# Reordered norms and layer ends, token sums of squares, and zero matmuls in a two-layer f32 decoder trunk

## What is computed

```python
def rms_norm(x, g):
    y = x * lax.rsqrt(jnp.mean(x * x, axis=-1, keepdims=True) + NORM_EPS)
    return y * g
def modulate(x, g, shift, scale):
    return rms_norm(x, g) * (1 + scale[:, None, :]) + shift[:, None, :]
...
for i in range(2):
    sh1, sc1, g1, sh2, sc2, g2 = jnp.split(silu(c) @ ada_w[i] + ada_b[i], 6, axis=-1)
    h = modulate(x, tok_norm[i], sh1, sc1)
    y = short_conv_mixer(h, ...) if i == 0 else mla_mixer(h, ...)
    x = x + g1[:, None, :] * y
    h = modulate(x, ch_norm[i], sh2, sc2)
    x = x + g2[:, None, :] * peer_mixer(h, peer_q_w[i], peer_subkeys[i], peer_u[i], peer_v[i])
```

## Time and profile before

| what | value |
| --- | --- |
| median of 3 runs | 2018.03 us (2015.09 to 2019.81) |
| the profiled execution's own time | 2020.03 us |
| its span, first to last instruction | 2018.3 us |
| PE busy | 94% of the span |
| DVE, ACT, POOL busy | 81%, 50%, 14% |
| mean granted TensorE clock | 0.972 of full |
| DMA | 371.70 MB, mean 184 GB/s |

### The profile page before, as it was taken

One profiled execution on the slowest core, in us unless ns is written; L12 is line 12 of the kernel. 1 busy time (PEld: TensorE's weight loads), 2 busy tenths in 40 slices (PEclk: granted clock), 3 DMA queues, 4 the chain that ended last, 5 costly groups with the idle time before them and its releaser, 6 DMA issues.

```text
span 2018.3 us, 39416 instructions
## 1 busy us (share of the span) xinstructions
PE 1893.6 (94%) x12830; PEld 1650.6 (82%) x12830; DVE 1633.7 (81%) x3102; ACT 1008.4 (50%) x1620; POOL 292.5 (14%) x171
## 2 busy tenths in 40 slices
PE   2989899999999999999878889899999999999998
PEld 2988888888888888888766789898888888888876
DVE  6747999999999999987755469998888888888866
ACT  3334355555555555554433344445555555555543
POOL 2866500000000000000043167000000000000000
PEclk7999999999999999999878899999999999999999
DMA  7964544776777777777523045435555555555553
GB/s 284 336 230 139 171 147 144 221 223 225 219 227 225 223 220 228 221 219 235 169 65 98 35 154 158 141 119 181 183 178 178 179 178 182 179 177 179 183 180 132
DMA packets 102179, 371.70 MB, mean 184 GB/s; under 512 B 11344, under 2 KB 11728, under 8 KB 101584
## 3 DMA queue, kind: packets, MB, share of 16 engines
q1 hardware_dynamic: 94032, 341.26, 52.7%
q0 software_dynamic: 8064, 29.36, 5.0%
HBM read 369.53 MB, written 1.05 MB: 184 GB/s over the span
## 4 chain that ended last, share of the span: by engine, by line
PE 79%; DVE 13%; DVEq 3%; issue 1%; ACT 1%; DMA 1%; POOL 1%; SPq 0%; ACTq 0%; POOLq 0%
PE bank L506 35%; PE bank L492 17%; PE bank L494 9%; PE bank L422 4%; PE bank L423 4%; PE bank L424 4%; DVE w_lo L1030 2%; PE bank L518 2%; DVE hot_b L1265 1%; DVEq L1271 1%; PE bank L662 1%; DVE arena L1156 1%; DVE arena L1136 1%; POOL w_lo L986 1%; DVE arena L1123 1%
## 5 line engine op out<-in xcount | busy, mean ns | idle before, releaser
L727 ACT CAST w_hi<-raw 128x1024 fp32r<-128x1024 f32 (+1 forms) x603 | 630.8, 1046 | 311.7 <-PE bank L506 113.8
L1030 DVE TENSOR_TENSOR w_lo<-raw,w_hi 128x1024 fp32r<-128x1024 f32 x493 | 603.3, 1224 | 134.8 <-PE bank L494 59.7
L492 PE MATMUL bank<-act_two,w_hi 128*128 128x512 f32 x1536 | 548.1, 397 | 0.0
L494 PE MATMUL bank<-act_two,w_lo 128*128 128x256 f32 x1536 | 430.6, 280 | 0.0
L422 PE MATMUL bank<-act_two,w_hi 128*128 128x256 f32 x1092 | 321.0, 294 | 39.1 <-DVE w_lo L1030 17.1
L492 PEld LDWEIGHTS bank<-act_two,w_hi 128*128 128x128 f32 x1536 | 288.6, 188 | 69.0
L506 PE MATMUL bank<-w_hi,wt_hi 128*128 128x512 f32 x1024 | 328.2, 401 | 3.3 <-DVE wt_lo L1304 2.6
L506 PE MATMUL bank<-w_lo,wt_hi 128*128 128x512 f32 x1024 | 318.9, 393 | 0.0
L506 PE MATMUL bank<-w_hi,wt_lo 128*128 128x512 f32 x1024 | 316.1, 390 | 0.0
L423 PE MATMUL bank<-act_two,w_hi 128*128 128x256 f32 x1092 | 312.9, 287 | 0.0
L424 PE MATMUL bank<-act_two,w_lo 128*128 128x256 f32 x1092 | 312.5, 286 | 0.0
(11 more groups left out here) (212 smaller groups left out, 1915.0 us busy)
## 6 DMA issues: line engine op xcount, KB each, us to landing
raw<-in_u_panels SPq DMA_DIRECT2D x256, 512.0 KB, 3.6
raw<-in_v_panels SPq DMA_DIRECT2D x256, 512.0 KB, 3.6
raw<-in_panels SPq DMA_DIRECT2D x81, 512.0 KB, 4.1
ada<-in_ada_rows POOLq DMA_DIRECT2D x56, 512.0 KB, 4.7
arena<-in_ada_rows SPq DMA_DIRECT2D x40, 512.0 KB, 6.1
raw<-in_panels SPq DMA_DIRECT2D x6, 384.0 KB, 3.0
arena<-in_subkeys SPq DMA_DIRECT2D x2, 1024.0 KB, 5.6
xT<-in_xT SPq DMA_DIRECT2D x1, 1024.0 KB, 8.1
```

What stands on the lines that cost most here:

```text
L492: pe.matmul(bank[:, 0:2 * T], w_hi[:, slots[0], w], act_two[:, :, a], start=(k == 0), stop=False, skip_group_check=True)
L494: mm = pe.matmul(bank[:, 0:T], w_lo[:, slots[1], w], act_hi[:, a], start=False, stop=(k == KB - 1), skip_group_check=True)
L727: nc.scalar.copy(w_hi[:, slot, 0:width], raw[:, slot, 0:width]).then_inc(hi_done, 1)
L1030: dve.tensor_tensor(w_lo[:, lo_slot, 0:width], raw[:, slot, 0:width], w_hi[:, slot, 0:width].bitcast(F32), ALU.subtract).then_inc(lo_done, 1)
```

## The change

Seven edits in one:

- **Norm.** `square_sums` becomes `token_square_sums`: the squares are the stationary operand and one column of ones is streamed, so the sums stand with tokens on the partitions, one column for each tile of 128 tokens. Root and reciprocal then have 128x2 elements. `spread_rstd` brings the reciprocal back to all partitions with one matmul per tile (the reciprocal broadcast as stationary operand, the identity streamed) into STAT in PSUM, from where `scale_x` reads it. `block_square_sum` changes in the same way.
- **Opening.** Six slots for the rows instead of four; SP loads one row, then `xT`, constants and vectors, then the other rows; ACT writes silu straight to `silu_c`, and all rows read it there; POOL does its first `w_lo` after its multiplication by the reciprocal, which ACT copies from PSUM for it.
- **End of conv_in.** The last two rows, `modulation` and the release of `conv_out` change places: the gate of the last block and the release come first.
- **gains.** `gain` is computed in the stage before instead of at the start of `peer` and `attention`.
- **residual_panels.** The split of a panel goes ahead of the wait for the residual and its square.
- **Layer end.** A semaphore after tile 0's half of the last value panel; ACT copies tile 0 there and half of tile 1, DVE the other half. The output is stored in four parts as they are done.
- **busy.** Matmuls of 512 columns with a zero stationary and a zero streamed operand, into banks that nobody reads then: 38 in the opening; 4, 2 and 4 around the norm of each `peer`; 18 after each search; 2 ahead of each group of transposes in layer 0; 3, 2 and 4 around the norm of `attention`, 36 after its `first_pair`, 26 ahead of `q_b`.

```diff
-ADA = 4
+ADA = 6
...
-            for j in range(2):
-                load_ada(j, KB + j, j)
+            load_ada(0, KB, 0)
             sp.dma_start(xT[:], xT_in).then_inc(s_const, 16)
-            for j in range(2, ADA):
-                load_ada(j, KB + j, j)
             sp.dma_start(con[:, 0:C_MASK], con_in[:, 0:C_MASK]).then_inc(s_const, 16)
             sp.dma_start(vec[:], vec_in).then_inc(s_const, 16)
-            for j in range(ADA, KB):
+            for j in range(1, KB):
                 load_ada(j, KB + j, j % ADA)
...
-            sp.wait_ge(x_ready, 4)
-            sp.dma_start(out, xT[:]).then_inc(s_out, 16)
+            for t in range(TT):
+                for g in range(2):
+                    sp.wait_ge(yt_added, 4 + 2 * t + g + 1)
+                    part = lambda a: a.rearrange("p (k t) -> p k t", t=T)[:, 4 * g:4 * g + 4, t * P:(t + 1) * P]
+                    sp.dma_start(part(out), part(xT[:])).then_inc(s_out, 16)
...
-                        mm = pe.matmul(STAT[:, t * P:(t + 1) * P], ones, sq[:, t * D + k * P:t * D + (k + 1) * P],
+                        mm = pe.matmul(STAT[:, t:t + 1], sq[:, t * D + k * P:t * D + (k + 1) * P], ones[:, 0:1],
...
             def block_square_sum(n):
                 pe.wait_ge(sq_summed, n // 2)
-                pe.matmul(STAT[:, 0:T], ones, sq_sum, start=True, stop=False)
                 pe.wait_ge(sq_block, KB * n // 2)
-                pe.matmul(STAT[:, 0:T], ones, sq[:, (KB - 1) * T:KB * T], start=False, stop=True).then_inc(sum_ready, 1)
+                for t in range(TT):
+                    o = (KB - 1) * T + t * P
+                    pe.matmul(STAT[:, t:t + 1], sq_sum[:, t * P:(t + 1) * P], ones[:, 0:1], start=True, stop=False)
+                    mm = pe.matmul(STAT[:, t:t + 1], sq[:, o:o + P], ones[:, 0:1], start=False, stop=True)
+                mm.then_inc(sum_ready, 1)
+
+            def spread_rstd(n):
+                pe.wait_ge(rstd_ready, n)
+                for t in range(TT):
+                    mm = pe.matmul(STAT[:, T + t * P:T + (t + 1) * P], rstd[:, t:t + 1].broadcast_to([P, P]), ident,
+                                   start=True, stop=True)
+                mm.then_inc(rstd_spread, 1)
+
+            def busy(bank, count):
+                for _ in range(count):
+                    pe.matmul(bank[:], zero[:], zero[:].unsqueeze(1).broadcast_to([P, 4, P]), start=True, stop=True)
...
             def peer(l):
+                busy(SC[0], 4)
                 block_square_sum(2 * l + 2)
+                busy(SC[0], 2)
+                spread_rstd(2 * l + 2)
+                busy(SC[0], 4)
...
+                busy(STAT, 18)
...
             def attention():
-                square_sums(3)
+                busy(SC[0], 3)
+                token_square_sums(3)
+                busy(SC[0], 2)
+                spread_rstd(3)
+                busy(SC[0], 4)
                 for j in range(7):
                     if j == 0:
                         first_pair(norm_hi, norm_ready, 2 * KB, [wait_panel("mla_in", p) for p in range(2)])
+                        busy(SC[0], 36)
...
                 latent_sums(STAT, 2, QB, KVB)
+                busy(SC[0], 26)
                 pe.wait_ge(act_ready, 1)
...
-            square_sums(1)
+            token_square_sums(1)
+            spread_rstd(1)
+            busy(PAN[0], 38)
             first_pair(norm_hi, norm_ready, 0, [wait_panel("conv_in", p) for p in range(2)])
...
             def residual_panels(stage, after):
                 for i in range(KB):
+                    split_hi(*((stage, i + HI_LEAD) if i + HI_LEAD < KB else (after, i + HI_LEAD - KB)))
                     act.wait_ge(evac[stage], i + 3)
                     c = slice(i * T, (i + 1) * T)
                     nc.scalar.activation(sq[:, c], xT[:, c], ACT.Square).then_inc(sq_block, 1)
-                    split_hi(*((stage, i + HI_LEAD) if i + HI_LEAD < KB else (after, i + HI_LEAD - KB)))
...
-                act.wait_ge(pan_done, ring(f"last{l}", 31)[3] + HI)
+                act.wait_ge(y0_done, l + 1)
                 for n in range(2):
                     i = nc.scalar.mul(yrow[:, n * 512:(n + 1) * 512], YB[n][:], 1.0 / G_SCALE)
                 i.then_inc(y0_copied, 1)
+                act.wait_ge(pan_done, ring(f"last{l}", 31)[3] + HI)
+                nc.scalar.mul(yrow[:, 2 * 512:3 * 512], YB[2][:], 1.0 / G_SCALE).then_inc(y1_copied, 1)
...
-            split_lo("conv_in", 0)
             pool.wait_ge(s_const, 48)
-            pool.wait_ge(rstd0, 1)
+            pool.wait_ge(rstd0_copied, 1)
...
             def inverse_rms(n):
                 dve.wait_ge(rms_ready, n)
-                dve.reciprocal(rstd[:, 0:T], rms[:, 0:T])
+                dve.reciprocal(rstd[:, 0:TT], rms[:, 0:TT]).then_inc(rstd_ready, 1)
...
             def scale_x(n):
+                dve.wait_ge(rstd_spread, n)
                 for k in range(KB):
                     c = slice(k * T, (k + 1) * T)
+                    dve.scalar_tensor_tensor(out=act32[:, c], in0=xT[:, c], scalar=gain[:, k:k + 1], in1=STAT[:, T:2 * T],
+                                             op0=ALU.mult, op1=ALU.mult).then_inc(scaled, 1)
...
+                    if end:
+                        dve.sem_inc(evac["conv_out"], 2)
+                        for k in range(KB // 2, KB):
+                            conv_low(k)
+                        ada_row(17 + 3 * b, 12, it, 3 * b + 1)
+                        ada_row(15 + 12, 12, it, 11)
```

More of the change, by code:

```diff
@@ L507, in v_panel @@
                                                start=False, stop=False, skip_group_check=True)
+                    if t == 0 and tile0 is not None:
+                        mm.then_inc(tile0, 1)
                 mm.then_inc(pan_done, 1)
@@ L584, in peer @@
                         v_panel(f"last{l}", 2 * s + 1, 4, it, s, 1)
+                for s in range(2):
+                    pe.wait_ge(wt_ready, 64 * l + 48 + 14 + s + 1)
+                    v_panel(f"last{l}", 2 * s, 4, 7, s, 0)
+                    v_panel(f"last{l}", 2 * s + 1, 4, 7, s, 1, y0_done if s else None)
                 for t in range(TT):
-                    pe.wait_ge((y0_copied, y1_copied)[t], l + 1)
+                    if t == 0:
+                        pe.wait_ge(y0_copied, l + 1)
+                    else:
+                        pe.wait_ge(y1_copied, 2 * (l + 1))
                     for g in range(2):
+                        if l == 0:
+                            busy(YB[0], 2)
                         if 2 * t + g >= 2:
@@ L880, in _ @@
             act.wait_ge(s_c, 16)
+            nc.scalar.activation(silu_c, crow[:], ACT.Silu).then_inc(s_silu, 1)
             nc.scalar.activation(crow[:], crow[:], ACT.Silu).then_inc(s_silu, 1)
-            act.wait_ge(s_silu, 1)
-            nc.scalar.copy(silu_c, crow[:]).then_inc(s_silu, 1)
             act.wait_ge(s_const, 48)
@@ L1342, in experts @@
                     mix_body(q, 7, True)
+                if l == 0:
+                    gains(1, V_TOK + KB, 0)
                 def last_body(it, end):
@@ L1377, in peer @@
             def peer(l):
-                gains(l, V_CH + l * KB, 3)
                 inverse_rms(2 * l + 2)
-                scale_x()
+                scale_x(2 * l + 2)
                 normalised_lo(2 * l + 2, l, 3)
@@ L1417, in attention @@
             def attention():
-                gains(1, V_TOK + KB, 0)
                 dve.sem_inc(evac["mla_in"], 2)
                 inverse_rms(3)
-                scale_x()
+                scale_x(3)
                 normalised_lo(3, 1, 0)
@@ L1506, in attention @@
                 dve.sem_inc(qk_ready, 1)
+                dve.sem_inc(evac["mla_out"], 2)
+                gains(1, V_CH + KB, 3)
                 for i in range(HEADS + 3):
@@ L1585, in _ @@
                                                  op0=ALU.mult, op1=ALU.add)
-                    ada_row(17 + 3 * b, 12, it, 3 * b + 1)
-                    if b == 3:
-                        ada_row(15 + 12, 12, it, 11)
+                    end = b == 3 and it == 1
+                    if not end:
+                        ada_row(17 + 3 * b, 12, it, 3 * b + 1)
+                        if b == 3:
+                            ada_row(15 + 12, 12, it, 11)
                     dve.drain()
@@ L1598, in _ @@
                         conv_low(b)
-            for k in range(KB // 2, KB):
-                conv_low(k)
+            gains(0, V_CH, 3)
             add_to_x("conv_out", 0, 1)
```

50 lines of the change are left out of this document (24 added, 26 removed).

## The result

| | before | after |
| --- | --- | --- |
| median of 4 runs each, one chip | 2017.05 us (2015.09 to 2019.81) | 1991.74 us (1988.87 to 1995.65) |
| ratio | | 0.9875, 95% interval 0.9854 to 0.9896 |
| profiled execution, span | 2020.03, 2018.3 us | 1992.0, 1989.6 us |
| mean granted clock | 0.972 | 0.989 |

What follows compares the result with a forecast made beforehand. PE was taken as the bound, with some 1400 us of expert stages fixed and 640 us between where it waits or runs at half clock. Terms summed to 26.4 us: 2018.03 - 26.4 = 1991.6 us, range 1986 to 2003.

Steps and rivals of the forecast that it cites:

- Opening: Start to conv_in's panel 2: earlier constants, unblocked rows and full clock gain 10.5 us (8.5 to 11.5).
- End of conv_in: Earlier release leaves PE waiting 2.8 us for POOL's split; with half the half-clock window, gain 3.3 us (2 to 4.7).
- third rival: In conv_in, late loads take up to 5 us of the opening's gain: 1997 us, chance 5%.
- Starts of PEER: Both PEER stages: first product 1.0 us sooner and panel 0 ending 1.5 sooner; 3.0 us for both (1.2 to 4).
- Start of attention: Norm at the end of layer 0: shorter chain, scale_x 4.0 us sooner; 3.5 us arrive (1.5 to 4.2).
- at full clock only 16 records stand behind the last squares: Attention's norm: those records take 1.9 us, so the sums end at 1000.7 instead of 1003.50.
- Clock behind it: Behind attention's start and ahead of q_b, zeros avoid half-clock matmuls (2.5 and 1.7): 4.2 us (1 to 4.5).
- Small ones: Minor terms: mla_out released early 0.3, zeros behind the searches -0.2, the end of the run 1.8 us.
- The 18 zeros: Fillers behind each search, where PE waits for DVE's w_lo: nothing gained, -0.2 us (-2 to 0).
- End: End of the run: adds begin 1.1 us sooner and the last quarter's store saves 0.7; 1.8 us (1.0 to 2.7).
- second rival: Zeros do not count as activity, so PE drops to 0.50 inside the fillers: 2024 us, chance 4%.
- first rival: The clock falls all the same despite the zeros; only the chains count, 17.3 us: 2000.7 us, chance 13%.

Runs made afterwards that it cites:

- the wide norm: The changed kernel with the old 256-wide norms in front of both PEERs and attention, opening and zeros as in the change: 1998.06 us, ratio 0.9896.
- e4_gain_later: The changed kernel, but in the opening DVE computes the first gain after row 9 instead of before row 8: 1992.02 us, ratio 0.9862.
- e7_72: The changed kernel with 72 zero matmuls behind the first_pair of mla_in in place of 36: 1997.58 us, ratio 0.9888.
- e9_more_zeros: The changed kernel with zeros at four more places (conv_out's first_pair, attention's scores, its last value weights, mla_out): 1986.41 us, ratio 0.9841.
- e10_both: The changed kernel with sums streaming 128 columns, zeros at four more places, 46 opening zeros and 8 between first_pair's halves: 1984.54 us, ratio 0.9827.
- e12_all: The e10_both kernel with the first gain read from PSUM and 48 opening zeros: 1983.16 us, ratio 0.9821.

## Why the prediction was right

The time was right to 0.1 us, the gain to 1.1 (25.3 for 26.4), the terms less so. The profiles differ by 28.0 us, 2.7 more than the medians, so the measured terms add up to more than 26.4.

- **Opening**, 10.5: 10.4 measured. Order, loads and blocked gain came as worked out, and of the clock's share 0.6 (43.9 us without zeros) where 1.0 was forecast. The experiments add that the six slots are 2 us of it.
- **End of conv_in**, 3.3: 3.1, of which 0.6 lie in the loop. The third rival was there in small: the wait was 3.4 us, not 2.8, because of a load.
- **Starts of PEER**, 3.0: 1.9 each, 3.7. The chain from the last square to the first product went from 4.63 us to 3.64 in front of both, the 1.0 forecast, and at PEER 0 it did so without zeros too. The rest is first_pair at full clock, 8.23 us for 9.09: 0.9 each where I had 0.5. The zeros alone bring just that at PEER 0 (8.26).
- **Start of attention**, 3.5: 4.9 (1.0 of it ahead of the last transposes). The failed step is "at full clock only 16 records stand behind the last squares": the clock fell in the midst of the sums (981.61), they ended 2.9 us behind the last square instead of 2.0, and `scale_x` began 4.8 us behind it. Before it was 6.5, forecast was 3.3, and with 128 columns streamed, which held the clock, it is 3.4. So of 3.2 us this chain brought 1.7. That the term came in all the same was luck: the layer end brought what was missing. From the first transposes to the end of the last square pass 5.95 us for 8.24 (6.17 without zeros), and 1.0 lies ahead of them, where I had counted 0.75 for all. The copies start earlier, and DVE's modulation of one column ahead of them, which ended with POOL's split (990.17 to 992.52), is now done before the split starts (974.52):

```profile
990.21 2.32 DVE L1047 TENSOR_TENSOR mod<-ada_sum,vec 128x1 f32<-128x1 f32 x1
...
974.19 0.16 DVE L1093 TENSOR_TENSOR mod<-ada_sum,vec 128x1 f32<-128x1 f32 x1
```

  On one-column records the Trainium skill (TensorE: Matmul & The Clock Gate, LDWEIGHTS) has it that a weight load is paid by its columns. The trace agrees in that one streamed column costs as much as 128, but the page's 107 ns fit only full clock (0.112 us a record); at half clock a record takes 0.213 (6.96 us for 32). The rule of the same page (PE-mode transpose) that transposes don't count for the clock did not decide here: with the transposes unchanged, two zeros ahead of each group of them, the clock held once the sums had 128 columns. No run shows transposes alone.
- **Clock behind it**, 4.2: 4.1, and 4.1 again as the loss of the run without zeros. The best-priced term, though the same stretch varies by 2.8 us between versions with the same code there (see the end of this section).
- **Small ones**: mla_out 0.3, nothing seen. The 18 zeros -0.2, nothing seen in the change; but its lower bound, -2, is what the old kernel with zeros and the wide norm paid, by DVE's additions and not by the `w_lo` that was priced. **End** 1.8: 2.5 (0.9 ahead of PE's last matmul, 1.6 behind it), since the span ended 2.7 us after the start of the last quarter's issue where I had 3.5 (4.2 for the whole).

The second rival, zeros that don't count as work, fell: the clock rose in the midst of the 38 (22.46).

What was wrong is the split, and that the sum came out is luck. My first rival, in which only the chains count, had 17.3 us; the chains alone brought 21. I had priced them as if every drop of the clock stayed where it was, and shorter waits removed some (conv_out's start in the run without zeros, 2.9 us over its 2.0 in the rival). The layer end brought 2.6 us more than I had given it. The zeros were priced at 9 and bring 4 to 6, by intervals that touch. Two errors of opposite sign gave 26.4.

Open: which of the small drops of the clock appears in which execution. The profiled runs took 87.9 to 90.6 us from panel 2 of mla_in to attention's transposes with the same code (the change; e4_gain_later). Of these 2.8 us, 1.5 are a drop at 1005.29, and 1.1 are no drop but the DVE operation shown with e7_72, which POOL's split holds in some runs and not in others. That this makes most of the scatter of 7 us is argued from the three versions with fewer drops (e9_more_zeros, e10_both, e12_all), whose runs lie within 1.0, 1.7 and 0.8 us; it was not shown run by run.

## What to carry to other kernels

Fill a wait of PE with matmuls of zeros only up to its length in the trace, and look for the places by the granted clock, not by PE's busy share, which the zeros blind. Price a small DVE operation with two operands in SBUF by what POOL does beside it; an operand in PSUM frees it (0.17 us for 3.76), though here the time saved was lost again to loads and to the clock. Where such an operation starts within a few hundredths of a us of POOL's, an edit elsewhere can turn 1 to 2 us on or off. And take a change apart even when the sum comes out: here the parts were off by some 4 us each way.

## What the runs showed of the hardware

- A DVE operation on 128x8 elements with both operands in SBUF took 3.76, 3.73 and 2.23 us, each time to within 0.03 us of the end of the POOL operation beside it (24.81, 28.53, 27.2); with one operand in PSUM, 0.17 in the same place. Rows of 128x1024 that read PSUM were not held (1.22 to 1.26). The Trainium skill (SBUF — State Buffer, Who interferes with whom) has it that a DVE instruction with two SBUF inputs and a GpSimd one that reads SBUF exclude each other, and that the order of issue decides who waits; the four numbers agree, and so do the additions in the search, free when they started 0.04 us ahead of POOL's split and held when 0.04 us behind. At 0.01 us ahead one operation was free in the change and held in e7_72.
- In the search the same group of four additions takes 0.50 us alone and up to 2.93 beside a split of POOL; over the 16 groups of the change it is 27.4 us, where 16 times 0.50 is 8, and each of the twelve groups that take over 1 us overlaps a split of POOL. Reading one operand from PSUM there was not tried.
- 32 matmuls of one column took 6.96 us, all at 0.50; of 128 columns 5.19, with the clock rising at 13.90. In the change it rose only in the zeros behind them. A record of either kind follows the last by 0.213 us at 0.50 and by 0.112 at 1.00.
- Matmuls of zeros raised the clock (at 22.46, behind 32 one-column records and in the midst of 38 zeros) and held it: with them q_b ran at 1.00, without them at 0.50 again.
